# Conditioning by pairs of channel blocks, used as they come by two projection units and the gates

## What is computed

```
mod = silu(c) @ ada_w + ada_b                  # 6 x 1024 values; shift and scale come first
u   = rmsnorm(x,   norm1_g) * (1 + scale)     + shift        # 256 latent tokens
uc  = rmsnorm(ctx, norm1_g) * (1 + scale_ctx) + shift_ctx    # 256 context tokens, from c_ctx
p   = u @ w_in,  pc = uc @ w_in               # q, k, v, gates (16 columns), o, dq, dk, dv, ...
g   = p[3] + gate_b                           # 4 heads x 2 directions: input and forget gates
logf = log_sigmoid(f_pre)
```

## Time and profile before

| | |
|---|---|
| median of 3 runs | 2528.64 us (2525.32 to 2531.08) |
| profiled execution | 2524.67 us |
| its span | 2522.9 us |
| TensorE busy in the span | 2321.1 us (92%) |
| VectorE, ScalarE, GpSimd busy | 1073.4, 590.4, 59.9 us |
| mean granted TensorE clock | 0.974 |
| DMA | 608.58 MB, mean 241 GB/s |

### The profile page before, as it was taken

The page is one execution under the profiler, slowest core; times in us unless marked ns, Lnnn a source line. Parts: engine busy times, 40 slices in busy tenths (PEclk is TensorE's granted clock), DMA queues, the critical chain, the costliest instruction groups (busy, mean ns, idle before and its releaser), DMA issues.

```text
span 2522.9 us, 35285 instructions
## 1 busy us (share of the span) xinstructions
PE 2321.1 (92%) x14214; PEld 1590.2 (63%) x14214; DVE 1073.4 (43%) x2311; ACT 590.4 (23%) x1417; POOL 59.9 (2%) x78
## 2 busy tenths in 40 slices
PE   7999998999998989979888677999999999999998
PEld 4898865686342423323333223878999898779997
DVE  2555646712121211111111012675875464676863
ACT  2000113511221111111111111462222223533221
POOL 1000000000000000000000000010000000010000
PEclk8999999999999999989999888999999999999999
DMA  8122353056999999899999999323343443223432
GB/s 343 67 101 100 134 217 117 34 219 237 386 419 421 417 421 417 366 421 421 421 421 421 421 420 378 129 89 134 134 149 123 164 158 142 84 76 142 155 122 109
DMA packets 86998, 608.58 MB, mean 241 GB/s; under 512 B 9568, under 2 KB 11744, under 8 KB 16144
## 3 DMA queue, kind: packets, MB, share of 16 engines
q1 hardware_dynamic: 86224, 602.49, 60.2%
q0 software_dynamic: 608, 3.78, 0.4%
HBM read 605.18 MB, written 1.05 MB: 240 GB/s over the span
## 4 chain that ended last, share of the span: by engine, by line
PE 73%; SPq 12%; DMA 7%; DVE 4%; issue 2%; ACT 2%; POOL 0%; PEldq 0%; DVEq 0%; POOLq 0%; PEld 0%; ACTq 0%
PE bank L590 16%; SPq L1084 12%; PE bank L2787 9%; PE bank L622 8%; PE bank L712 7%; PE bank L3135 6%; DMA ring<-in_w_e 4%; PE bank L3140 3%; PE bank L3159 3%; PE bank L692 3%; DMA arena<-in_w_e 2%; PE bank L3168 2%; PE bank L3075 1%; PE bank L2873 1%; PE bank L3338 1%
## 5 line engine op out<-in xcount | busy, mean ns | idle before, releaser
L590 PE MATMUL bank<-arena,ring 128*128 128x272 f32 (+2 forms) x1792 | 410.2, 389 | 4.6 <-DMA ring<-in_w_proj 2.1
L590 PEld LDWEIGHTS bank<-arena,ring 128*128 128x128 f32 x1792 | 339.3, 191 | 65.5 <-DMA ring<-in_w_proj 2.5
L2119 DVE TENSOR_TENSOR arena<-bank,arena 128x256 f32<-128x256 f32 x56 | 23.8, 425 | 772.5 <-PE bank L3108 748.5
L2264 DVE SCALAR_TENSOR_TENSOR arena<-arena,par 128x272 f32<-128x272 f32 (+1 forms) x272 | 134.3, 496 | 82.2 <-ACT arena L1689 46.5
L3135 PE MATMUL bank<-arena 128*64 128x512 f32 x616 | 149.4, 612 | 8.8 <-DMA arena<-in_w_e 8.6
L3140 PE MATMUL bank<-arena 128*32 128x512 f32 x800 | 112.3, 648 | 38.5 <-DMA arena<-in_w_e 38.5
L2787 PE MATMUL bank<-arena 128*128 128x256 f32 (+1 forms) x704 | 130.2, 341 | 0.0
L2787 PEld LDWEIGHTS bank<-arena 128*128 128x128 f32 x704 | 114.5, 191 | 11.6
L622 PE MATMUL bank<-arena 128*128 128x129 f32 (+1 forms) x960 | 113.7, 277 | 0.0
L622 PEld LDWEIGHTS bank<-arena 128*128 128x128 f32 x960 | 111.1, 191 | 0.0
L712 PE MATMUL bank<-arena 128*128 128x136 f32 (+2 forms) x912 | 105.7, 277 | 0.0
(11 more groups left out here) (519 smaller groups left out, 3376.8 us busy)
## 6 DMA issues: line engine op xcount, KB each, us to landing
arena<-in_w_e SPq DMA_DIRECT2D x207, 1024.0 KB, 25.6
ring<-in_w_e SPq DMA_DIRECT2D x151, 1024.0 KB, 25.2
ring<-in_w_up SPq DMA_DIRECT2D x44, 1024.0 KB, 4.8
ring<-in_w_l SPq DMA_DIRECT2D x37, 1024.0 KB, 4.8
con<-in_w_e SPq DMA_DIRECT2D x26, 1024.0 KB, 26.1
ring<-in_w_ada SPq DMA_DIRECT2D x24, 1024.0 KB, 6.2
ring<-in_w_proj SPq DMA_DIRECT2D x24, 1024.0 KB, 5.4
ring<-in_w_down SPq DMA_DIRECT2D x32, 704.0 KB, 4.2
```

The source lines that it names most:

```text
L590: mm = pe.matmul(o[:, a:n], ring[:, s, k * 256 + c * P:k * 256 + (c + 1) * P], rhs(k), start=(k == 0), stop=(k == KT - 1))
L2264: ins = dve.scalar_tensor_tensor(out=dst, in0=src[:, a + k:k + L], scalar=w(k), in1=dst, op0=ALU.mult, op1=ALU.add)
```

## The change

It replaces what stands ahead of the wide units. The first eight units of `w_ada` are cut the other way: two units ("pieces") hold all input channels of 512 output columns, which are the shift and scale of two channel blocks. After each pair of pieces ScalarE copies 512 columns, TensorE sums and turns them by four products with a constant of ones (`pick`), and VectorE and ScalarE finish u for these two blocks, latent and context. These blocks are used at once: by the first projection unit of q, which has a place of its own (`w_first`, where km lies later) and a DMA of its own, and by half of the gates' products after the fourth block. The second unit of q follows from the ring with the last blocks of both. The gates are now eight products with the 32 gate columns stationary and 512 tokens streamed, in four column groups, then a copy by ScalarE and four turning products (`gate_turn`), which stand in the middle of wide unit 0. The context's squares are summed by eight products on TensorE instead of by GpSimd. The halves of u are made by pairs of blocks. The stream has one unit fewer; GpSimd loads `wg` at once and the other constants when nine units have been used.

```diff
-        stream = units_of("w_ada", 0, KT) + units_of("w_proj", 0, 24)
+        stream = units_of("w_ada", 0, KT) + units_of("w_proj", 1, 24)
...
+            sp.dma_start(ctxT[:, :, :], dram["ctxT"]).then_inc(sem("ctx_step"), 16)
             for n, (src, width) in enumerate(stream):
-                if n == KT:
-                    sp.dma_start(ctxT[:, :, :], dram["ctxT"]).then_inc(sem("x_loaded"), 16)
+                if n == 2:
+                    sp.wait_ge(sem("x_loaded"), 16)
+                    sp.dma_start(w_first, dram["w_proj"][0]).then_inc(sem("x_loaded"), 16)
                 fill(n, src, width)
...
+            act.wait_ge(sem("ctx_step"), 16 + KT + 1)
+            act.activation(rs[:, T:2 * T], bank[:, 4, 0:T], ACT.Sqrt, bias=cst("eps"), scale=1.0 / D)\
+               .then_inc(sem("ctx_step"), 1)
+            piece_copy(0)
+            for p in range(1, KT // 2):
+                piece_copy(p)
+                shifted(2 * p - 2)
+                shifted(2 * p - 1)
+            shifted(KT - 2)
+            shifted(KT - 1)
...
+            for k in range(KT):
+                dve.wait_ge(sem("ada_turned"), k // 2 + 1)
+                turned = bank[:, 2 + k // 2 % 2, 4 * k:4 * k + 4]
+                dve.tensor_scalar(mod[:, k, :], turned[:, 0:2], prm("ada_b", k), None, ALU.add)
+                chain(dve.scalar_tensor_tensor(out=A1[:, :, k], in0=turned[:, 2:4], scalar=scale_bias[:, k:k + 1],
+                                               in1=prm("norm1_g", k).to_broadcast([P, 2]), op0=ALU.add, op1=ALU.mult))
+                for j, rows_in in ((0, xT), (1, ctxT)):
+                    if (k, j) == (0, 1):
+                        dve.wait_ge(sem("ctx_step"), 16 + KT + 2)
+                        chain(dve.reciprocal(rs[:, T:2 * T], rs[:, T:2 * T]))
+                    dve.scalar_tensor_tensor(out=u[:, k, j * T:(j + 1) * T], in0=rows_in[:, k, :], scalar=A1[:, j, k:k + 1],
+                                             in1=rs[:, j * T:(j + 1) * T], op0=ALU.mult, op1=ALU.mult).then_inc(sem("u_scaled"), 1)
+                if k in (2, 4, 6):
+                    halves_part(k // 2 - 1)
+            halves_part(KT // 2 - 1)
+            wide_weights(0)
...
-            for k in range(1, KT):
-                pool.wait_ge(sem("ctx_step"), KT + k - 1)
-                pool.tensor_tensor(squares[:, 0, T:2 * T], squares[:, 0, T:2 * T], squares[:, k, T:2 * T], ALU.add)\
-                    .then_inc(sem("ctx_step"), 1)
...
-            project(pe, at, 1, u_lat, T, first=lambda k: pe.wait_ge(sem("u_ready"), k + 1))
...
-            project(pe, at, 1, u_lat, T)
...
-            for t in range(4):
-                for k in range(KT):
-                    mm = pe.matmul(bank[:, 4, t * 16:(t + 1) * 16], u_tok(k, t), wg[:, k, :],
-                                   start=(k == 0), stop=(k == KT - 1))
+            def gate_turn():
+
+                pe.wait_ge(sem("gate_step"), 2)
+                for t in range(4):
+                    mm = pe.matmul(bank[:, 4, t * 16:(t + 1) * 16], gate_rows[:, t * P:(t + 1) * P], cst("pick")[:, 0:16],
+                                   start=True, stop=True)
+                mm.then_inc(sem("gate_step"), 1)
...
+            for p in range(1, KT // 2):
+                piece(2 * p)
+                piece(2 * p + 1)
+                first_products(0, w_first, 2 * p - 2)
+                piece_turn(p)
+                first_products(0, w_first, 2 * p - 1)
+                if p == 2:
+                    gate_products(0)
+            w_second = ring[:, slot_filled(pe, at), :]
+            for k in range(KT - 2):
+                first_products(1, w_second, k)
+            for c in range(2):
+                for second, w in enumerate((w_first, w_second)):
+                    for k in (KT - 2, KT - 1):
+                        mm = first_products(second, w, k, (c,))
...
+            gate_products(1).then_inc(sem("gate_step"), 1)
...
-                middle = None
+                middle = gate_turn if i == 0 else None
```

More of the change, by code:

```diff
@@ new lines, in piece_turn, with first_products @@
+            def piece_turn(p):
+                pe.wait_ge(sem("ada_copied"), p + 2)
+                if p >= 2:
+                    pe.wait_ge(sem("u_scaled"), 4 * p - 5)
+                for c in range(4):
+                    mm = pe.matmul(bank[:, 2 + p % 2, 8 * p + 2 * c:8 * p + 2 * c + 2], pieces(p)[:, c * P:(c + 1) * P],
+                                   cst("pick")[:, 0:17:16], start=True, stop=True)
+                mm.then_inc(sem("ada_turned"), 1)
+            def first_products(second, w, k, columns=(0, 1)):
+                pe.wait_ge(sem("u_ready"), 2 * k + 1)
+                for c in columns:
+                    mm = pe.matmul(first_out[c][:, second * T:(second + 1) * T], w[:, k * 256 + c * P:k * 256 + (c + 1) * P], u_lat(k),
+                                   start=(k == 0 and not second), stop=(k == KT - 1), skip_group_check=True)
+                return mm
@@ new lines, in gate_products @@
+            def gate_products(part):
+                pe.wait_ge(sem("u_ready"), 8 * part + 8)
+                for q in range(4):
+                    k = 4 * part + q
+                    mm = pe.matmul(bank[q * 32:(q + 1) * 32, 4, :], wg[:, k, :], u[:, k, :],
+                                   start=(part == 0), stop=(part == 1))
+                return mm
+            def gate_turn():
[4 more added lines that the diff above has]
+                mm.then_inc(sem("gate_step"), 1)
@@ new lines, in _ @@
+            pe.wait_ge(sem("ones_loaded"), 16)
+            for k in range(KT):
+                pe.wait_ge(sem("squares"), k + 1)
+                mm = pe.matmul(bank[:, NB_NORM, 0:T], ones, squares[:, k, 0:T], start=(k == 0), stop=(k == KT - 1))
+            mm.then_inc(sem("norm_sum"), 1)
+            at.norm += KT
+            pe.wait_ge(sem("ada_copied"), 1)
+            piece(0)
+            for k in range(KT):
+                pe.wait_ge(sem("ctx_step"), 16 + k + 1)
+                mm = pe.matmul(bank[:, 4, 0:T], ones, squares[:, k, T:2 * T], start=(k == 0), stop=(k == KT - 1))
@@ new lines, in _ @@
+            mm.then_inc(sem("ctx_step"), 1)
+            piece(1)
+            piece_turn(0)
+            first_out = [out_bank(pe, at) for c in range(2)]
+            pe.wait_ge(sem("con_loaded"), 16)
+            pe.wait_ge(sem("x_loaded"), 32)
+            for p in range(1, KT // 2):
[6 more added lines that the diff above has]
+                    gate_products(0)
```

160 lines of the change are left out of this document (77 added, 83 removed).

## The result

| | before (beside it) | after |
|---|---|---|
| median (range, runs) | 2526.66 us (2522.91 to 2531.08, 10) | 2532.21 us (2527.71 to 2536.83, 10) |
| ratio, 95% interval | | 1.0022 [1.0014, 1.0030] |
| profiled execution, its span | 2524.67, 2522.9 us | 2527.71, 2525.9 us |
| mean granted clock | 0.974 | 0.971 |

The changed kernel is slower by some 5.5 us where 2.7 us of gain were forecast. The forecast time was 2525.9, and 2532.21 lies just outside the range.

A forecast was written before the change was run, and what follows sets the result against it. DMA was taken to bound the first units, then TensorE, with the expert stage DMA-bound. At wide unit 1, 75.73 - 71.15 - 1.85 = 2.7 us gained, so 2528.64 - 2.7 = 2525.9 us, range 2520.0 to 2532.0.

The forecast's parts named there:

- First piece: DMA at the start: the first piece lands at 15.1 us, behind one more megabyte and the gates' 128 KB.
- Norms of the context: Start: TensorE's eight products summing the context's squares follow ScalarE's squaring and end at 21.5 us.
- Pairs' ends: Loop over pairs of pieces at the start: ends at 26.1, 31.7 and 38.3 us.
- Wide unit 0: TensorE, after q and the gates' products: starts at 51.8 us, 9.9 us earlier than 61.72 before.
- Gates on VectorE: VectorE starts the gates after gate_turn, at 61.5 us, as late as before (61.91).
- Wide unit 1: TensorE waits 6.2 us for VectorE's first step of wide unit 0's results, then starts at 71.15 us.
- Clock lost behind the stall: After TensorE's wait ahead of wide unit 1 the clock is taken as lost, priced at 1.85 us.
- The queue had room at the experts' entry: Expert stage's entry: DMA idle share of 0.32, 3.2 us, hides one megabyte coming up to 2.47 us late.
- Rivals 1, 2 and 4: 1: cheaper stall, 5.1 to 6.5 us gain, 0.20; 2: no stall, 2518, 0.06; 4: no effect, within main case.
- the sum: At the start of wide unit 1: 75.73 - 71.15 - 1.85 = 2.7 us gained.
- What is won at the second wide unit should thus be won at the end: Stages behind the start: they move as one, so the whole 2.7 us gain reaches the end.
- rival 3: Clock falls in the loop over pairs: wide unit 0 up to 20 us late, 2546; 0.14 beyond the bound, 0.02 within.

The follow-up runs named there:

- cuts: Kernels before, changed and with the early turn, stopped at the first barrier, fourth barrier or behind the experts; before: 410.11, 512.33, 1569.52 us; changed: 411.06, 516.51, 1576.09 us.
- layout or slots alone: Kernel before with the changed kernel's memory layout (2529.09 us), or with five unused stream units turning its ring slots as the change does (2529.35 us).
- turn_early: Changed kernel with gate_turn behind the fourth product of wide unit 0 instead of the twentieth; 2525.22 us, ratio 0.9990 to the kernel before.
- combined: Changed kernel with gate_turn behind the fourth product, filler products in the loop's three waits and one unused unit turning slots back; 2521.73 us, ratio 0.9975.

## Why the prediction was wrong

**Right, with its numbers.** First piece at 15.1 us: 15.64. Norms of the context 21.5: 21.64. Pairs' ends 26.1, 31.7, 38.3: 26.3, 32.1, 38.8. Wide unit 0 at 51.8: 52.39. Gates on VectorE at 61.5: 62.19. Wide unit 1 at 71.15 behind 6.2 us of idle time: 72.09 behind 6.46. Clock lost behind the stall, 1.85 us by the first units of q: 1.82. The gain at that place was 1.8 us instead of 2.7. After the wait the products ran at 0.50. The trace thus agrees with the rule that the prediction takes from the Trainium skill ("TensorE: Matmul & The Clock Gate", "HAM oscillation — how this bites in real kernels"). The queue had room at the experts' entry, as forecast: the window at 630 to 640 us moves 0.66 of its capacity, before 0.68, and 0.3 of the lead of 0.4 us are still there at 650 us. Rivals 1, 2 and 4 did not come: wide unit 0 started after 49.4 us, and there was a stall.

**The step that failed** is the one sentence ahead of the sum, "What is won at the second wide unit should thus be won at the end". It was argued from the DMA queue at the experts' entry alone. In its place the first pair of traces shows the lead of 1.8 us turn into 3.0 us behind, at three places: 1.4 us at the opening of the two-map attention, 2.1 us in the expert stage (all of it behind its entry), 1.3 us in a break of TensorE's run behind the experts. The cuts' medians go the same way, +1.0, +4.2 and +6.6 us at the first barrier, the fourth and behind the experts. The last two are clear of zero (resampled, 0.3 to 7 and 3 to 14 us), the steps between them are not.

Of the attention the place is shown, and that both a longer wait and a longer low clock stand there; 2.9 us went behind the wait in the cuts' traces and 1.1 in the first two whole ones. Which of them brings the other is not shown. The wait of 2.68 in place of 2.32 us comes ahead of the fall in every kernel with the new start, but layout or slots alone also took the mean clock from 0.96 to 0.92 once each, without it, and both together did not. The Trainium skill ("TensorE: Matmul & The Clock Gate", "A second HAM failure mode: psum-queue depth-cycling") tells of short idle times between groups of products that come often enough to make the clock go up and down. The trace agrees in kind: the idle times there are 0.27 to 2.68 us, and none is as long as the 6.46 us of the stall.

For the expert stage the cause stays open. Its clock is low in many short stretches in every kernel, 0.90 in 1300 to 1575 us in the profiled run before and 0.86 to 0.89 in all other whole ones, those with the old start too. From the router to the first unit behind the experts the four whole traces with the new start and the late turn lose 1.3 to 2.1 us against the one of before, and the four others with the old start lose 1.1 to 5.2 as well. So much of what the first two traces differ in there is that the one of before was a good one.

**A mis-sized term** is the lead itself. The sum took 75.73 us, a single execution's place of wide unit 1, as the kernel's; eight traces of the old start scatter there from 72.84 to 78.25 us, and by the averages of the traces nothing is gained in the start where 2.7 us were forecast. The clock in the start is a part of this. The prediction charged it once, 1.85 us, and the first trace has 1.82; in the cut kernels the same products lost 2.9 to 3.0 us. Of rival 3, which would have the clock fall in the loop over pairs, the mechanism was seen in three of six traces at 1.6 us, all of cut kernels; its forecast of up to 17 was ten times too much, because each fall ended within twelve records.

**What fell of the other theories.** The second block's turned slot (16.4 us of a later issue) and the break in the instruction stream were both visible, and both moved as expected when turned or shifted. Neither is needed for the loss: the cut behind the experts has 6.6 us of it without either of them. But the break takes 1.3 us in the first pair of whole traces, and the layout and the slots may hold some 2 us; this rival is not excluded.

**The sign.** By the cuts' medians turn_early is 7.0 us ahead at the first barrier and 2.0 at the end, so 5.0 are lost behind it (resampled, 1.5 to 8); the changed kernel is 1.0 behind there and 5.5 at the end, so 4.5 (0.3 to 8). That the two tolls are nearly equal may be chance, for the traces place them differently: in turn_early and combined 6.3 us go in one fall of the clock in the first expert, which the changed kernel's traces do not have. Both were slow executions of their kernels (the slowest of 12 and of 10), so how often this fall comes is not known.

## What to carry to other kernels

When an edit shifts a start without changing the work behind it, do not carry the lead to the end. Look for every later stage in which TensorE waits in short intervals or works on narrow products, and put some us of either sign on each; a granted clock of 1.00 in the one trace of before is no promise for the next, as the first expert shows. To find where a small loss arises, compare the starts of equal instructions in two traces place by place, and time both kernels cut at common barriers, with more than five runs each: the cuts say what the kernels do on the whole, the traces what happened in one execution. A small step (here 0.96 us of turning products) that another engine's long chain hangs on belongs as early in the stream as its operands allow; moving it by sixteen products won 7.9 us.

## What the runs showed of the hardware

The clock of the same stretch of instructions falls in one trace and not in the next. In six traces of the changed start wide unit 1 began between 71.65 and 75.28 us and its first twelve products took 6.81 to 8.32 us; in eight of the old start it began between 72.84 and 78.25 us. In the first expert the same products took 11.9 us before and 18.2 with the early turn, with no wait of TensorE inside them; narrow products (32x32) and an idle time of 0.8 us preceded them in both. The series of whole kernels scatter by 4 to 13 us from run to run.

A run of products on TensorE can be broken by 0.3 to 2.6 us that nothing in the profile releases, at a place that depends on how many instructions came before: behind 14 records 0.42 us, behind 8 or 9 2.27 and 1.86. Three added products moved it by six records. In the two traces compared above the larger break was still there at the end of the span.

Fillers cost nothing while they filled waits: thirteen products of constants (26 records, 5.78 us) ended 0.84 us ahead of the release that TensorE was waiting for anyway, and the clock behind them was 1.00 instead of 0.50.
